# Feature blocks of the two hybrid layers' projections as seven half products in place of eight

## What is computed

```python
u = rms_norm(h, norm_g)
proj = jnp.einsum('bld,dp->blp', u, w_in)
dq, dk, dv, dz, fq, fk, fv, fz, f_logit = jnp.split(proj, split_points, axis=-1)
```

## Time and profile before

| | before |
|---|---|
| median of 3 runs | 3495.38 us (3483.2 to 3512.91) |
| the profiled execution | 3494.12 us, its span 3492.3 us |
| TensorE busy in the span | 3079.4 us, 88% |
| VectorE busy | 1549.9 us, 44% |
| the two projection stages | 258.0 and 260.0 us |

### The profile page before, as it was taken

How to read it: one execution, slowest core, us unless ns; L and a number is a source line. 1 busy time by engine, 2 the same in 40 slices (tenths; PEclk the granted TensorE clock), 3 DMA queues, 4 the chain that set the end, 5 groups by cost and what they waited for, 6 DMA issues and landing times. The chain is left out here.

```text
span 3492.3 us, 72027 instructions
## 1 busy us (share of the span) xinstructions
PE 3079.4 (88%) x31680; PEld 1769.2 (51%) x31680; DVE 1549.9 (44%) x3357; ACT 821.8 (24%) x1867; POOL 302.9 (9%) x311
## 2 busy tenths in 40 slices
PE   6998999989799999599999979998998877777777
PEld 5855658546344564333333335557888853322222
DVE  4574536656554581411212154238888863211111
ACT  2113410124211470100000010147766530000000
POOL 0001000000111110000000000001222220000000
PEclk9998999999899999799999989989999998899999
DMA  6564136720320311599999932100000034899998
GB/s 184 154 198 152 25 88 156 200 89 25 111 72 33 89 51 73 205 372 375 380 374 381 376 121 74 41 1 5 5 5 5 5 120 170 313 395 405 398 398 347
DMA packets 149735, 608.69 MB, mean 174 GB/s; under 512 B 17616, under 2 KB 20240, under 8 KB 132912
## 3 DMA queue, kind: packets, MB, share of 16 engines
q1 hardware_dynamic: 143280, 583.12, 46.1%
q0 software_dynamic: 6144, 20.98, 2.5%
HBM read 578.23 MB, written 32.11 MB: 175 GB/s over the span
## 5 line engine op out<-in xcount | busy, mean ns | idle before, releaser
L1922 PE MATMUL psum<-ring,big 128*32 128x256 f32 (+1 forms) x5280 | 691.3, 478 | 60.3 <-DMA ring<-moe_w 46.3
L1922 PEld LDWEIGHTS psum<-ring,big 128*32 128x32 f32 (+1 forms) x5280 | 244.2, 122 | 495.3 <-issue 367.5
L2022 DVE TENSOR_TENSOR big<-big,psum 128x512 f32<-128x512 f32 (+1 forms) x48 | 28.7, 599 | 617.4 <-PE psum L1922 617.4
L414 PE MATMUL psum<-h_uT,ring 128*128 128x264 f32 x1280 | 290.5, 387 | 0.0
L543 DVE SCALAR_TENSOR_TENSOR h_O<-h_O,cond_silu 128x512 f32<-128x512 f32 x336 | 226.8, 743 | 105.5 <-DMA h_O<-ada_w 105.4
L414 PEld LDWEIGHTS psum<-h_uT,ring 128*128 128x128 f32 x1280 | 242.0, 190 | 46.5 <-issue 5.8
L1922 PE MATMUL psum<-big 128*64 128x512 f32 x864 | 205.1, 621 | 56.3 <-DMA big<-moe_w 44.3
L2033 DVE SCALAR_TENSOR_TENSOR big<-psum,gate,gates 64x512 f32<-64x512 f32 (+1 forms) x128 | 78.8, 615 | 249.2 <-PE psum L1922 247.8
L2492 PE MATMUL psum<-ring,gates 64*64 64x128 f32 (+1 forms) x5120 | 167.5, 253 | 5.4 <-issue 3.8
L1985 ACT ACTIVATE big<-psum 128x512 f32<-128x512 f32 (+1 forms) x48 | 23.5, 524 | 623.5 <-PE psum L1922 623.5
L434 PE MATMUL psum<-ring,h_uT 128*128 128x512 f32 x384 | 169.8, 600 | 0.0
(11 more groups left out here) (378 smaller groups left out, 4658.7 us busy)
## 6 DMA issues: line engine op xcount, KB each, us to landing
ring<-moe_w SPq DMA_DIRECT2D x138, 2048.0 KB, 11.6
big<-moe_w SPq DMA_DIRECT2D x54, 2048.0 KB, 31.5
h_O<-ada_w SPq DMA_DIRECT2D x192, 256.0 KB, 2.9
ring<-w_in SPq DMA_DIRECT2D x16, 2048.0 KB, 13.1
ring<-na_w_qkv SPq DMA_DIRECT2D x6, 2048.0 KB, 8.2
ring<-w_out SPq DMA_DIRECT2D x4, 2048.0 KB, 8.9
bias_rows<-na_table SPq DMA_DIRECT2D x16, 480.0 KB, 14.2
sums<-X SPq DMA_DIRECT2D x12, 512.0 KB, 5.9
```

What stands on the lines that cost most here:

```text
L414: last = nc.tensor.matmul(bank(k, pair_bank(q) + h, NH), w[:, a, f * P:(f + 1) * P], uT[:, a, halves[h]], start=a == 0, stop=a == KD - 1)
L1922: last = nc.tensor.matmul(bank(k, b, r.width)[q * r.n:(q + 1) * r.n, :], rowsT[:, half * HALF_K + n, r.first:r.first + r.n], w[:, n, q * r ...
L2022: nc.vector.tensor_tensor(hid[:, wide(r)], silu[:, wide(r)], bank(k, r.gates, r.width), ALU.mult).then_inc(s.hid_ready, 1)
```

## The change

The feature blocks are taken in pairs (0 with 4, 1 with 5, ...; 8 with 12, ...; 16 with 18, 17 with 19), so that a pair is 2 blocks of features by 2 halves of the tokens, each a product over 2 halves of the contraction: eight half products of 4 matmuls. Winograd's form of Strassen's scheme makes them from seven half products, P1 to P7, of sums of weight quarters (S1 to S4) and of token quarters (T1 to T4). Ten pairs, so 280 matmuls of 264 columns in place of 320 in a stage.

- VectorE makes the sums: at the stage's start S3, S1, S2 (128x2048 each), T1 to T4 (128x1056 each), S4 (128x2048), ahead of anything else; S1 to S4 again for the second group of pairs, and in half the size for the third. It also adds the products up: seven additions of 128x264 out of PSUM for a pair. ScalarE copies only P1 out of PSUM, scales, and applies silu.
- T1 to T4 lie in V and S3 in Z, which are filled later. S2 and S4 lie in X, the residual, which is therefore stored to DRAM at the stage's start (four DMAs of 512 KB) and loaded again behind the last `w_in` chunk.
- A product takes one bank, banks 2 to 7 go round singly, and a bank is free when VectorE has added it in.
- The modulations' units are spread anew: 44 beside the products (at most one after a product), 52 beside the row tiles (5 per tile).
- The ring's chunks are issued at other steps: when P2 of the group's last pair is done and S4 made, and when its last P3 is done.

The core of the diff:

```diff
+            if q == 0:
+                count = kind in ("P7", "P4", "P3") or kind == "P6" and x >= 2
+            elif q == 1:
+                count = kind in ("P6", "P7", "P4", "P3") or kind == "P2"
+            else:
+                count = kind in ("P2", "P6", "P7", "P4", "P3")
...
+    T1, T2, T3, T4 = (quarters(n) for n in range(4))
+    saved = k.X[:, 0:LT, :].rearrange("p a b -> p (a b)")
...
+            for t in range(LT):
+                sp.dma_start(k.sums[t * P:(t + 1) * P, :], k.X[:, t, :]).then_inc(s.saved, 16)
             for u in range(MOD_BUFS):
                 load_unit(u)
...
+                if kind == "P3" and x in last_of:
+                    q = last_of.index(x)
+                    sp.wait_ge(s.P3, x + 1)
+                    load_chunk(k, sp, c0 + SLOTS + (1, 3, 4)[q])
+                    if q == 2:
+                        for t in range(LT):
+                            sp.dma_start(k.X[:, t, :], k.sums[t * P:(t + 1) * P, :]).then_inc(s.restored, 16)
...
+            def product(kind, g, left, right, done):
+                banks_free((kind, g))
+                q = BLOCK_PAIRS[g][2]
+                i = g - (last_of[q - 1] + 1 if q else 0)
+                for a in range(half):
+                    last = nc.tensor.matmul(got(kind, g), left[:, a, i * P:(i + 1) * P], right[:, a, :], start=a == 0, stop=a == half - 1)
+                last.then_inc(done, 1)
...
+                elif kind == "P4":
+                    dve.wait_ge(s.P4, j + 1)
+                    dve.wait_ge(s.u3, j + 1)
+                    nc.vector.tensor_tensor(place(j, 1, 0), place(j, 1, 1), got(kind, j), ALU.add).then_inc(s.c21, 1)
+                    if j in last_of[:2]:
+                        weights(last_of.index(j) + 1, 0)
...
+            weights(0, 0)
+            nc.vector.tensor_tensor(T1, B12, B11, ALU.subtract).then_inc(s.tokens, 1)
+            dve.wait_ge(s.tokens, 1)
+            nc.vector.tensor_tensor(T2, B22, T1, ALU.subtract).then_inc(s.tokens, 1)
+            nc.vector.tensor_tensor(T3, B22, B12, ALU.subtract).then_inc(s.tokens, 1)
+            dve.wait_ge(s.tokens, 2)
+            nc.vector.tensor_tensor(T4, B21, T2, ALU.subtract).then_inc(s.tokens, 1)
+            weights(0, 1)
             lambdas()
```

More of the change, by code:

```diff
@@ L280, in mod_schedule @@
     units, n = {}, 0
-    for q, (kind, j) in enumerate(order):
+    for step, (kind, x) in enumerate(order):
         count = 0
[L283 to L288, removed]
+        if kind == "rows":
+            if HTILES[x % len(HTILES)][1] == P:
+                count = 5
+        elif kind != "mirror":
+            q = BLOCK_PAIRS[x][2]
+            if q == 0:
[4 more added lines that the diff above has]
+                count = kind in ("P2", "P6", "P7", "P4", "P3")
+        units[step] = list(range(n, min(n + int(count), MOD_UNITS)))
+        n += len(units[step])
     assert n == MOD_UNITS
     made = {}
-    for q, mine in units.items():
+    for step, mine in units.items():
         for u in mine:
             if u % KD == KD - 1:
-                made.setdefault(q + 1, []).append(u // KD)
+                made.setdefault(step + 1, []).append(u // KD)
     return units, made
@@ L310, in hybrid_project @@
     meta_cols = lambda q: slice(q * CHUNK // META_PARTS, (q + 1) * CHUNK // META_PARTS)
[L312 to L317, removed]
+    FIRST_BANK, BANKS_IN = 2, 6
+    half = KD // 2
+    NG = len(BLOCK_PAIRS)
+    bank_of, before, owner, n = {}, {}, {}, 0
@@ new lines, in hybrid_project @@
+    for step in order:
+        wide = 2 if step[0] == "mirror" else 1
+        bank_of[step] = [FIRST_BANK + (n + h) % BANKS_IN for h in range(wide)]
+        before[step] = [owner[b] for b in bank_of[step] if b in owner]
+        for b in bank_of[step]:
+            owner[b] = step
+        n += wide
+    last_of = [max(g for g, x in enumerate(BLOCK_PAIRS) if x[2] == q) for q in range(3)]
+    first_half, second_half = slice(0, half), slice(half, KD)
+    B11, B12, B21, B22 = (uT[:, rows, cols] for rows in (first_half, second_half) for cols in halves)
@@ L418, in mirror, with banks_free @@
-            def mirror(q, j):
-                pair_free(q)
-                pe.wait_ge(s.out_done, j + 1)
+                last.then_inc(s.logits_made, 1)
+            emptied = {"P1": s.kept, "P2": s.c11, "P6": s.u2, "P7": s.u3, "P4": s.c21, "P5": s.w12, "P3": s.c12, "mirror": s.mirror_out,
+                       "rows": s.rows_out}
+            def banks_free(step):
+                for kind, x in before[step]:
+                    pe.wait_ge(emptied[kind], mirror_turn(x) + 1 if kind == "mirror" else x + 1)
@@ L421, in mirror @@
                 for h in range(2):
-                    last = nc.tensor.matmul(bank(k, pair_bank(q) + h, NH), k.rope_mirror[:, :], qkT[:, j, halves[h]],
-                                            start=True, stop=True)
-                last.then_inc(s.product, 1)
+                    last = nc.tensor.matmul(bank(k, bank_of["mirror", j][h], NH), k.rope_mirror[:, :], qkT[:, j, halves[h]], start=True, stop=True)
+                last.then_inc(s.mirrored, 1)
             def row_tile(j):
@@ L563, in _ @@
+                for u in units[step]:
                     weigh(u)
[L564 removed]
+                for n in made.get(step - 1, ()):
                     mod_out(n)
```

238 lines of the change are left out of this document (170 added, 68 removed).

## The result

The changed kernel takes 3559.25 us (median of 4 runs, 3555.55 to 3568.62), the kernel before beside it on the same chip 3499.16 (4 runs, 3483.2 to 3512.91): ratio 1.0169, interval 1.0148 to 1.0191. It is slower, by about the 60 us forecast. The profiled execution took 3555.55 us.

The account below looks back on a forecast made before the run. VectorE and the DMA ahead of it were taken to bound the kernel: features 173, rows 111 and clock 5 make 289 us per stage against 259, so 3494.12 + 60 = 3554 us, range 3515 to 3592.

Parts of the forecast that it names:

- TensorE's saving: Products: 40 matmuls fewer at 0.445 us save 17.8 us per stage, 35.6 in all, 1.0% at most.
- VectorE's new work: Per stage: additions and sums add 54.7 us to 145.9, making 200.6; with DMA waits 254, against TensorE's 242.
- Stage start: Start of each stage: sums and the store of X delay ScalarE's copy of P1; P6 begins at 25 us.
- Features: Features part: 25 start, 121 VectorE work, 15 for two chunks, 12 waiting for products: 173 us against 160.
- Bound (b): VectorE's 12 us of waiting for products could be 0 or 20: -24 to +16 us over both stages.
- Rows: Rows part: units 70, `mod_out` 3, chunk and residual 17, `w_out` chunks 11, late start and end: 111 us against 98.9.
- Clock: Seven TensorE waits over 3 us per stage bring the lower clock: 12 us slower, about 5 not hidden behind VectorE.
- VectorE's waits for `ada_w` should still be 40 us or more.: Sign to look for, per stage: VectorE's waits for units' loads stay that long, the longest behind the residual's load.
- Rival 1: Both parts: lists mesh, VectorE never waits for products; stage 257 us, 3490 in all; 3470 to 3530 has chance 0.17.
- Rival 2: TensorE still sets the pace if units land within some 7 us of a chunk: 3466 us; chance 0.04.
- Rival 3: Late units, late chunks and TensorE's lower clock feed each other: +45 us per stage, 3584, up to 3600; chance 0.09.

Follow-up runs that it names:

- the last kernel: Changed kernel with later sums, chunks in four DMAs, lambda reductions before the eight sums, residual reloaded behind second `w_out` chunk, units respread: 3470.29 us, 0.9916 of kernel before.
- the late sums: Changed kernel with each `mod_sum` beside the products four steps later in TensorE's list: 3514.09 us, 1.0058 of the kernel before.
- without parking: Changed kernel with the store of X and its reload left out (residual then not right): 3532.22 us, 1.0124 of the kernel before.
- parts alone: Changed kernel with each 2 MB chunk and the residual's reload as four DMAs between units' loads, sums not moved: 3524.37 us, 1.0057 of the kernel before.
- the kernel before with parts: Kernel before the change with its chunks in four parts between the units: 3490.51 us, 0.9977 of the kernel before.

## Why the prediction was right

**Direction, size and place** held: 3554 forecast, 3559.25 measured, features 173 against 175.6 and 181.1, rows 111 against 109.9 and 110.3. The mechanism held in part. That TensorE would wait for VectorE, and VectorE for the DMAs, came true; that VectorE would be the bound did not: it waited for products twice as long as forecast, and moving the sums alone, with all of its work in place, gave back 17.6 and 19.6 us a stage. By its steps:

- **TensorE's saving, 17.8 us a stage.** The products' matmuls are recorded 1120 times, and from the product at 62.99 to the next at 64.77 (timeline below) are 1.78 us, for four matmuls the 0.445 each of before. In the last kernel, with TensorE nearly always busy, the features part has 143.12 us of work, against 142.7 by the prediction's step.
- **VectorE's new work, 54.7 us** to a total of 200.6. Measured 199.3 and 199.4. One addition:

```profile
L700 DVE TENSOR_TENSOR h_qkT<-h_qkT,psum x16: 422/428/430, 57.6 to 614.4; 128x264 f32<-128x264 f32 x16
```

428 ns, as the earlier trace rows. But the conclusion that I drew, VectorE "becomes the bound before any wait on TensorE is counted", was too strong: the additions' load alone cost some 6 us a stage, and with the same load the last kernel gains.
- **Stage start.** P6 began 27.1 us into the stage (forecast 25), the copy of P1 held TensorE for 4.40 and 6.02 us (4.5):

```profile
45.14 2.29 DVE L678 TENSOR_TENSOR X<-ring 128x2048 f32<-128x2048 f32 x1 [4.51 <-DMA sums<-X]
...
57.67 5.49 PE L488 MATMUL psum<-h_uT,ring 128*128 128x264 f32 x16 [4.40 <-ACT h_qkT L578]
...
62.99 1.94 PE L488 MATMUL psum<-h_V,X 128*128 128x264 f32 x8
...
64.77 1.50 PE L488 MATMUL psum<-h_V,h_Z 128*128 128x264 f32 x6
```

- **Features, the step that was right in sum and wrong in its split.** Behind the start the terms were 121 us of VectorE's work, 15 for two chunks and 12 for products, 148 in all. Behind P6 are 148.5 us in layer 0 and 154.0 in layer 1; VectorE was busy in them for 113.6 and 113.4, waited 8.2 and 14.8 for units and 24.5 and 23.9 for products. The work was overstated by 7: an addition had 0.385 us, half of a pair's 0.77, while in the timeline above the instruction behind the one at 88.64 starts 0.34 later, which is 3 us over 66; a unit took 1.30 (87.34 to 88.64) in place of 1.35, another 2; and one unit and one addition ran only in the rows part. The chunks were overstated by 7 in layer 0 and right in layer 1. The waits for products were understated by 12: "TensorE waits on banks and in `mod_sum`" gave a price to neither. The banks, on which most of the reasoning rests, cost TensorE 2.5 us; `mod_sum` cost it 16.8 and 23.4, and the late sums took 19.7 and 22.6 us off the features. Bound (b) let the waits for products grow to 20 a stage, and they passed it. That the errors cancelled is luck.
- **Rows.** 17 for chunk and residual (14.9 and 15.3 measured), 11 for the two `w_out` chunks (11.3 and 12.5). The last sum kept VectorE waiting for 10.0 and 8.9, where a row tile of 7.13 and a store had been put. This step held nearly term by term, and without parking 5 of the 15 go.
- **Clock.** 5 us a stage were put down for it. Every stretch shows a granted clock of 0.92, and TensorE's busy time is 9.1 and 7.2 us above 142.7 and 141.8 in the features, 4.7 and 3.4 above before in the rows: 13.8 and 10.6 us in each stage, where I had 12, of which 5 uncovered. The stretches around the wait of 4.91 us shown above:

```profile
87.20:92.00 4.80, 0.00 (x0) 0.00 (x0) 4.80 (x10) 0.00 (x0) 0.00 (x0) 0.72 0.31 77
92.00:95.40 3.40, 3.31 (x13) 2.05 (x14) 2.04 (x5) 0.00 (x0) 0.00 (x0) 0.50 0.44 129
```

4.8 us idle, then 0.50 for 3.4 us, which is 1.2 GHz, as the earlier trace rows had it. The Trainium skill, TensorE: Matmul & The Clock Gate, Part 1, has it that an idle TensorE falls to the lower clock and must first be busy again; these rows agree.
- **"VectorE's waits for `ada_w` should still be 40 us or more."** 34.4 in layer 0, a miss; 42.6 in layer 1. The longest stands behind the residual, as said, 14.9 and 15.3.
- **Rivals.** Rival 1, that the lists mesh, did not come by itself; the edits of the sums' place and the chunks' size bring about its time (3501.68), though VectorE still waits for some products there. Rival 2 named one condition, the hold behind a chunk, for a faster kernel; with parts alone the ratio is still 1.0057, so that condition was not enough. The last kernel has the sums' place and the units' spread as well.
- **Rival 3**, worse feedback with +45 a stage, stayed away in size (+27.5 and +31.4), though the clock's 13.8 us in layer 0 passed the full 12 that it assumed.

What stays open: why the features of layer 1 wait 6.6 us longer for the same units than those of layer 0, and why the spread helps layer 0 by 11.1 us and layer 1 by 3.5.

## What to carry to other kernels

Count where two engines' lists wait for each other, not only each one's work: a consumer that stands one short step behind its last producer can cost a wait each time (here in four sums of the features part), and moving it a few steps back took them away for 2 to 3 us more in the next part. A change that shortens the steps between such points (7.1 us per feature to 1.8 per product) needs them moved. Large background DMAs beside small ones that are due should go in pieces between them; 512 KB is the only size that was tried. And a saving in matmuls is to be weighed against the old form with the same edits: here 0.4% over the kernel before shrank to next to nothing over the kernel before with parts, and 17.5 us of the last kernel's gain stood up to it.

## What the runs showed of the hardware

- A chunk of 2 MB ahead of loads of 256 KB on one queue held the next unit back by 12.1 to 17.6 us from its issue (`w_in`) or 8.8 (`w_out`), about what a chunk itself takes to land in the median, 13.1 and 8.9, though 2 MB at 397 GB/s are 5.3 us; with the residual's 2 MB behind it 19.8 and 20.3. As four DMAs of 512 KB with units between them, no wait was over 2.7 us (changed kernel) and the sum fell from 34.4 to 19.5 in layer 0. In the kernel before the longest fell only from 13.2 to 7.0 and the sum from 53.4 to 37.9 (layer 1); it gained 5.5 and 4.6 us a stage by it.
- 54 us of additions a stage on VectorE, with nothing of TensorE's features waiting on them, left TensorE's features part about as it was (158.4 and 160.8 against 160.6 and 159.6); the rows part grew by 8.2 and 4.5.
- Operations of VectorE that follow each other overlap at their ends: an addition of 128x264 out of PSUM takes 428 ns from start to end, and the next instruction starts 0.34 us after it did.
